# Expert weights fetched as pairs of slices, two neighbouring rows of DRAM per partition, with the gather and the transposes reading every second column

## The chip, the cores and the metric

One NeuronCore of a Trainium2 chip. The metric is the device time of one execution in microseconds; the kernel before takes 1547.8 us (median of 3 runs, 1546.68 to 1548.04).

## The reference

Two transformer blocks over 256 tokens of width 1024, all in float32. The first has window attention, retention and a convolutional feed-forward; the second has differential and banded attention and then the part that the change touches, a mixture of 32 experts of which each token takes 4:

```
logits = t @ w_router + b_router            # t: 256 x 1024
top_val, top_idx = lax.top_k(logits, 4);  gate_w = softmax(top_val)
for each expert e, over the tokens that chose it:
    hb = x_e @ w_exp_in[e] + b_exp_in[e]    # w_exp_in[e]: 1024 x 2048, 8 MB
    g = min(hb[:, :1024], 7);  u = clip(hb[:, 1024:], -7, 7)
    a = g * sigmoid(1.702 * g) * (u + 1)
    y_e = a @ w_exp_out[e] + b_exp_out[e]   # w_exp_out[e]: 1024 x 1024, 4 MB
y[token] = sum over its 4 experts of gate_w * y_e
```

## The kernel before

The kernel is written engine by engine, each with its own list of instructions, held together by semaphores. Everything up to the router takes about 580 us of the span; then a loop runs over the 32 experts in an order that the device works out itself (`order`, sorted by the number of tokens and then mixed). All of the second part's expert weights pass through one buffer: `win` holds eight slices `win[:, k, :]` of 2048 columns, `wout` eight slices of 1024 columns. Slice k of `win` holds rows 128k to 128k+127 of the expert's matrix, one row on each partition (L311 and L312), and comes by one transfer of 1 MB; a slice of `wout` is 0.5 MB.

SP issues all these transfers. For expert 0 it sends sixteen at once (L384 to L387), as soon as the attention part has left the memory. After that `expert` (L393) refills each slice as soon as it is consumed: it waits until PE has counted `gu_part` (for `win`, L400) or `y_part` (for `wout`, L403) once more, and sends the slice of the next expert to the place that has come free (L401, L404). So SP runs up to one whole expert ahead of PE, and the order in its queue is win 0 to 7, wout 0 to 7, win 0 to 7 of the next expert, and so on.

PE does for an expert, in `one_pass` (L942): the bias and eight slices of the first product (`gu`, L855; L873 waits for the slice's own semaphore, L863 are the matmuls, with the gathered tokens `xT` as the stationary operand and the weights moving), a part of the gather for the next expert (`gather`, L841; L846: the stationary operand is `h1`, 128 of its 1024 columns for each k, the moving one a selection matrix `picks`), transposes for the way back (L883), transposes of the activations `a` (`turn_a`, L886; L891), eight slices of the second product (`second`, L894; L897 waits, L902 are the matmuls), and the addition to the tokens (`combine`, L916 or L925). Each slice is counted on `gu_part` (L878) or `y_part` (L906) behind its last matmul.

Tokens come in blocks (`GROUPS`, L36): an expert with up to 32 tokens has one block of 32, up to 64 one block of 64, beyond that both. In this input 19 experts have the small block, 9 the large, and 4 both. An fp32 matmul is shown as two instructions; a slice of `win` is 8 of them with either block, and 16 with both. DVE and ACT make `picks`, the copies of the gathered tokens and the swiglu (L1816 to L1823, L1335, L1339, L1348) beside it.

Of the kernel before, what the change touches and what calls it, by code (L numbers as in the profile page):

```python
# [16 lines left out]
P = 128  # L17
D = 1024
SEQ = 256
T = SEQ // P  # L20
KD = D // P
# [10 lines left out]
SLOTS = TRIO * XS  # L32
# [89 lines left out]
def program(nc, ins, out):  # L122
# [2 lines left out]

    with ExitStack() as ctx:
        s = {n: ctx.enter_context(nc.semaphore(n)) for n in EVENTS}
        win_in = [ctx.enter_context(nc.semaphore(f"win{k}_in")) for k in range(KD)]
        wout_in = [ctx.enter_context(nc.semaphore(f"wout{k}_in")) for k in range(KD)]


        ring_mem = ctx.enter_context(nc.sbuf_tensor("ring_mem", [P, 3 * 4096], F32))
# [24 lines left out]
        def carve(mem, places):  # L157
# [18 lines left out]
        win = big_mem[:, 0:KD * 2 * FE].rearrange("p (k n) -> p k n", k=KD)  # L176
        wout = big_mem[:, KD * 2 * FE:].rearrange("p (k n) -> p k n", k=KD)
# [16 lines left out]
        at = sum(int(np.prod(m2[n].shape[1:])) for n in ("score", "turned", "qaT", "kaT", "va", "qbT", "kbT", "vb", "gateT"))  # L194
        toep_flipped = big_mem[:, at:at + BAND_HEADS * SEQ].rearrange("p (h k) -> p h k", h=BAND_HEADS)
        moe = carve(ring_mem, [
            ("xT", (KD, SLOTS)), ("g", (TRIO * QW,)), ("sig", (TRIO * QW,)), ("u", (TRIO * QW,)),
            ("a", (TRIO * QW,)), ("y", (TRIO * QW,)), ("pairs", (E, E)), ("part", (SEQ,)), ("chosen", (T, 4 * E))])
# [8 lines left out]
        h1 = h  # L207
# [44 lines left out]
        ident = stay[:, IDENT:IDENT + P]  # L252
# [4 lines left out]
        ps = ctx.enter_context(nc.psum_tensor("ps", [P, 8, 512], F32))  # L257
# [50 lines left out]

        cw = ins["conv_w"][0].rearrange("w (f p) -> (w f) p", p=P)
        mix1_cols = [(0, 512), (512, 256), (768, 512), (1280, 512), (1792, 512), (2304, 512)]  # L310
        win_x = ins["w_exp_in_2"].rearrange("l e (k p) n -> (l e) k p n", p=P)  # L311
        wout_x = ins["w_exp_out_2"].rearrange("l e (k p) n -> (l e) k p n", p=P)  # L312


        @block.sync
        def _(sp):
# [64 lines left out]
                sp.dma_start(moe["bias"][E * part:E * (part + 1), 0:2 * FE], ins["b_exp_in_2"][0]).then_inc(s["bias_in"], 16)  # L381
            sp.dma_start(moe["bias"][0:E, 2 * FE:], ins["b_exp_out_2"][0]).then_inc(s["bias_in"], 16)
            sp.wait_ge(s["merged_ready"], KD)
            for k in range(KD):  # L384
                sp.dma_start(win[:, k, :], win_x[0, k]).then_inc(win_in[k], 16)
            for k in range(KD):
                sp.dma_start(wout[:, k, :], wout_x[0, k]).then_inc(wout_in[k], 16)  # L387

            sp.wait_ge(s["counts_ready"], 1)
            done = sp.alloc_register("sp_done")  # L390
# [2 lines left out]
            def expert(before, cur):  # L393

                more = sp.value_load(further[0:1, 1, before], min_val=0, max_val=PASSES - 1)
                sp.reg_add(done, done, more)
                others = sp.snap(done, min_val=0, max_val=2 * TURNS)
                sp.reg_add(done, done, 1)
                for k in range(KD):
                    sp.wait_ge(s["gu_part"], KD * others + 1 + k)  # L400
                    sp.dma_start(win[:, k, :], win_x[cur, k]).then_inc(win_in[k], 16)  # L401
                for k in range(KD):
                    sp.wait_ge(s["y_part"], KD * others + 1 + k)  # L403
                    sp.dma_start(wout[:, k, :], wout_x[cur, k]).then_inc(wout_in[k], 16)  # L404

            expert(slice(0, 1), 1)
            sp.wait_ge(s["order_ready"], 1)
# [28 lines left out]
        def _(pe):  # L436
            mm = nc.tensor.matmul
# [119 lines left out]
            for g in range(2):  # L557
                for k in range(KD):
                    for z in range(2):
                        mm(ps[HEAD * z:HEAD * (z + 1), 2, SEQ * g:SEQ * (g + 1)], cols8[1][:, k, HEAD * g:HEAD * (g + 1)], hT[:, k, :],  # L560
                           start=(k == 0), stop=(k == KD - 1))
            for t in range(T):
                for k in range(KD):
                    last = mm(ps[:, 3, P * t:P * (t + 1)], hT[:, k, P * t:P * (t + 1)], cols8[1][:, k, P:2 * P],
                              start=(k == 0), stop=(k == KD - 1))
# [68 lines left out]
            for t in range(T):  # L634
                last = mixed(0, t, 4, KD)
# [45 lines left out]
            for k in range(NF - 4, NF):  # L681
                pe.wait_ge(s[f"lo{k % 4}"], NF // 2 + k // 4 + 1)
                last = down(k, 0)
# [157 lines left out]
            def gather(lo, hi, bank=7):  # L841

                for k in range(lo, hi):
                    c = SLOTS * (k % EARLY)
                    for t in range(T):
                        last = mm(ps[:, bank, c:c + SLOTS], h1[:, t, P * k:P * (k + 1)], moe["picks"][:, t, :], start=(t == 0), stop=(t == T - 1))  # L846
                if hi in (EARLY, KD):
                    last.then_inc(s["gather_ps"], 1)

# [5 lines left out]
            def gu(blocks, landed_all, tokens_all):  # L855

                def each(at, m, stationary, weights, start, stop):
                    w = D * m // P
                    bank = 4 + at // XS
                    for q in range(P // m):  # L860
                        for f in range(2 if m > XS else 1):
                            out = ps[m * q:m * (q + 1), bank + f, :] if m > XS else ps[m * q:m * (q + 1), bank, :].rearrange("p (f n) -> p f n", f=2)
                            last = mm(out, stationary, weights[:, f, w * q:w * (q + 1)] if m > XS else weights[:, :, w * q:w * (q + 1)], start=start, stop=stop)  # L863
                    return last

                if len(blocks) > 1:
                    pe.wait_ge(s["xT_ready"], tokens_all)
                for at, m in blocks:
                    each(at, m, own[:, 0:m], bias_gu, True, False)
                for k in range(KD):  # L870
                    if k == EARLY:
                        pe.wait_ge(s["xT_ready"], tokens_all)
                    pe.wait_ge(win_in[k], landed_all)  # L873
                    for b, (at, m) in in_turn(blocks, k):
                        last = each(at, m, moe["xT"][:, k, at:at + m], win[:, k, :].rearrange("p (f n) -> p f n", f=2), False, k == KD - 1)
                        if k == KD - 1 and b < len(blocks) - 1:
                            last.then_inc(s["gu_early"], 1)
                    last.then_inc(s["gu_part"], 1)  # L878
# [7 lines left out]
            def turn_a(at, m):  # L886

                w = D * m // P
                for c in range(w // P):
                    place = ps[:, 5, P * c:P * (c + 1)] if m > XS else ps[:, 4 + at // XS, SEQ + P * c:SEQ + P * (c + 1)]  # L890
                    last = nc.tensor.transpose(place, moe["a"][:, KD * at + P * c:KD * at + P * (c + 1)], ident)  # L891
                last.then_inc(s["aT_ps"], 1)

            def second(blocks, landed_all):  # L894

                for k in range(KD):
                    pe.wait_ge(wout_in[k], landed_all)  # L897
                    for b, (at, m) in in_turn(blocks, k):
                        w, n = D * m // P, m // 16
                        aT = aT_all[:, KD * at:KD * at + w].rearrange("p (c q m) -> p c q m", q=P // m, m=m)  # L900
                        for q in range(P // m):
                            last = mm(ps[m * q:m * (q + 1), 4 + at // XS, 0:w], aT[:, k % n, k // n, :], wout[:, k, w * q:w * (q + 1)],  # L902
                                      start=(k == 0), stop=(k == KD - 1))
                        if k == KD - 1 and b < len(blocks) - 1:
                            last.then_inc(s["y_early"], 1)
                    last.then_inc(s["y_part"], 1)  # L906
# [1035 lines left out]
```

## Time and profile before

| | |
|---|---|
| median of 3 runs | 1547.8 us (1546.68 to 1548.04) |
| the profiled execution | 1548.02 us, its span 1545.4 us |
| PE busy | 1358.8 us (88%) |
| DVE, ACT, POOL busy | 425.2, 331.7, 121.4 us |
| moved by DMA | 494.35 MB, mean 320 GB/s |
| of it expert weights | 256 transfers of 1 MB and 256 of 0.5 MB |

The trace shows one execution. Times are microseconds from the start of the span; the span is shorter than the execution by what lies before its first and behind its last instruction. PE is the matmul side of TensorE, PEld its weight loads, which run beside the matmuls. SPq and ACTq are the queues that issue transfers. The stretch from 583 us to 1530 us is the loop over the experts, over 60% of the span; the layer norm and the output follow in the last 15 us.

### The profile page before, as it was taken

How to read it: one execution, taken by the hardware profiler on the slowest of the kernel's cores; microseconds unless marked ns; L12 is line 12 of the kernel's file. 1: busy time of each engine (PE TensorE's matmuls, PEld its weight loads, DVE VectorE, ACT ScalarE, POOL GpSimd, SP SyncE). 2: the span in 40 equal slices, each digit the busy share in tenths (PEclk: the TensorE clock that was granted, in tenths of full speed). 3: DMA queues.
4: the chain of work that ended last, by engine and by line, in shares of the span. 5: the costliest groups of instructions: out<-in, count | busy, mean ns of one | idle time of the engine just before them, and what ended most of it. 6: DMA issues, size and time to landing. Idle time of an engine off the chain costs nothing.

```text
span 1545.4 us, 25866 instructions
## 1 busy us (share of the span) xinstructions
PE 1358.8 (88%) x9234; PEld 788.9 (51%) x9235; DVE 425.2 (28%) x892; ACT 331.7 (21%) x638; POOL 121.4 (8%) x56
## 2 busy tenths in 40 slices
PE   7998999998899998998988788988889988879874
PEld 5554999887789744442343243343323433333421
DVE  0336687753543262111021111111111111111112
ACT  2233566534555211000010010010000101000000
POOL 0000112005665000000000000000000000000000
PEclk9999999999999999999999998999999999999997
DMA  9341366855343198999999999999999999999995
GB/s 334 131 142 55 109 179 188 312 191 183 111 164 134 68 368 326 370 419 418 415 419 418 417 417 418 419 416 420 418 417 417 418 420 415 420 418 417 417 418 241
DMA packets 150051, 494.35 MB, mean 320 GB/s; under 512 B 11665, under 2 KB 59137, under 8 KB 117025
## 3 DMA queue, kind: packets, MB, share of 16 engines
q1 hardware_dynamic: 148531, 491.52, 81.1%
q10 hardware_dynamic: 1486, 2.34, 0.4%
q8 instruction: 25, 0.41, 0.1%
q14 instruction: 9, 0.07, 0.0%
HBM read 492.76 MB, written 1.06 MB: 320 GB/s over the span
## 4 chain that ended last, share of the span: by engine, by line
PE 58%; DMA 19%; SPq 12%; DVE 4%; issue 3%; ACT 3%; ACTq 0%; DVEq 0%
DMA big_mem<-in_w_exp_in 13%; PE ps L863 12%; SPq L404 8%; PE ps L902 6%; DMA big_mem<-in_w_exp_out 6%; PE ps L644 5%; PE ps L645 5%; PE ps L646 5%; PE ps L846 5%; PE ps L477 4%; SPq L401 3%; PE ps L774 2%; PE ps L782 2%; PE ps L616 2%; PE ps L668 1%
## 5 line engine op out<-in xcount | busy, mean ns | idle before, releaser
L863 PE MATMUL ps<-big_mem,ring_mem 128*32 128x512 f32 (+1 forms) x2304 | 391.9, 647 | 63.4 <-DMA big_mem<-in_w_exp_in 63.4
L863 PEld LDWEIGHTS ps<-big_mem,ring_mem 128*32 128x32 f32 (+1 forms) x2304 | 107.5, 124 | 321.3 <-issue 197.0
L902 PE MATMUL ps<-big_mem,x 128*32 128x256 f32 (+1 forms) x1888 | 183.3, 430 | 12.8 <-DMA big_mem<-in_w_exp_out 8.1
L644 PE MATMUL ps<-hT_hi,w_hi 128*128 128x256 f32 x600 | 172.0, 287 | 1.1 <-DVE hT_lo L1422 1.1
L645 PE MATMUL ps<-hT_lo,w_hi 128*128 128x256 f32 x600 | 171.1, 285 | 0.0
L646 PE MATMUL ps<-hT_hi,w_lo 128*128 128x256 f32 x600 | 171.0, 285 | 0.0
L846 PEld LDWEIGHTS ps<-ring_mem,h 128*128 128x128 f32 x1056 | 135.6, 202 | 64.6 <-issue 63.5
L846 PE MATMUL ps<-ring_mem,h 128*128 128x96 f32 x1056 | 153.5, 292 | 0.6 <-DVE ring_mem L1775 0.6
L1816 DVE TENSOR_SCALAR ring_mem<-ps 128x256 f32<-128x256 f32 (+1 forms) x36 | 18.7, 520 | 438.8 <-PE ps L863 438.8
L902 PEld LDWEIGHTS ps<-big_mem,x 128*32 128x32 f32 (+1 forms) x1888 | 69.6, 115 | 112.7 <-issue 64.8
L1335 ACT ACTIVATE ring_mem<-ring_mem 128x256 f32<-128x256 f32 (+1 forms) x36 | 17.7, 493 | 497.9 <-DVE ring_mem L1816 497.9
L644 PEld LDWEIGHTS ps<-hT_hi,w_hi 128*128 128x128 f32 x600 | 116.6, 194 | 3.8 <-issue 2.3
L645 PEld LDWEIGHTS ps<-hT_lo,w_hi 128*128 128x128 f32 x600 | 116.6, 194 | 0.0
L646 PEld LDWEIGHTS ps<-hT_hi,w_lo 128*128 128x128 f32 x600 | 116.5, 194 | 0.0
L1339 ACT ACTIVATE ring_mem<-ps 128x480 f32<-128x480 f32 x66 | 32.5, 492 | 354.2 <-PE ps L846 354.2
L429 POOL TENSOR_TENSOR w_lo<-ring_mem,w_hi 128x1024 fp32r<-128x1024 f32 x38 | 91.2, 2408 | 126.4 <-ACT w_hi L1222 126.4
L1832 DVE COPY ring_mem<-ps 128x256 f32<-128x256 f32 (+1 forms) x36 | 18.4, 520 | 269.4 <-PE ps L902 269.4
L477 PE MATMUL ps<-ring_mem,hT 128*128 128x512 f32 x128 | 56.0, 595 | 0.0
L1806 DVE TENSOR_SCALAR ring_mem<-stay,posb,gate 128x128 f32<-128x128 f32 x72 | 21.4, 344 | 103.6 <-PE ps L846 85.5
L1222 ACT ACTIVATE w_hi<-ring_mem 128x1024 fp32r<-128x1024 f32 x39 | 40.9, 1056 | 33.7 <-PE ps L646 27.7
L1148 ACT ACTIVATE w_hi<-ring_mem 128x1024 fp32r<-128x1024 f32 x44 | 44.9, 1050 | 0.0
L424 POOL TENSOR_TENSOR w_lo<-ring_mem,w_hi 128x1024 fp32r<-128x1024 f32 x11 | 26.8, 2441 | 219.6 <-ACT w_hi L1148 219.6
(284 smaller groups left out, 1328.0 us busy)
## 6 DMA issues: line engine op xcount, KB each, us to landing
big_mem<-in_w_exp_in SPq DMA_DIRECT2D x256, 1024.0 KB, 19.4
big_mem<-in_w_exp_out SPq DMA_DIRECT2D x256, 512.0 KB, 19.0
ring_mem<-in_w_in SPq DMA_DIRECT2D x15, 2048.0 KB, 8.0
ring_mem<-in_w_up SPq DMA_DIRECT2D x44, 512.0 KB, 4.9
ring_mem<-in_w_down SPq DMA_DIRECT2D x5, 2048.0 KB, 8.7
ring_mem<-in_w_out SPq DMA_DIRECT2D x4, 2048.0 KB, 8.7
ring_mem<-in_w_branch_a SPq DMA_DIRECT2D x1, 2048.0 KB, 7.5
ring_mem<-in_w_branch_b SPq DMA_DIRECT2D x1, 2048.0 KB, 7.4
```

The costliest lines, as they stand in the source:

```text
L401: sp.dma_start(win[:, k, :], win_x[cur, k]).then_inc(win_in[k], 16)
L404: sp.dma_start(wout[:, k, :], wout_x[cur, k]).then_inc(wout_in[k], 16)
L429: nc.gpsimd.tensor_tensor(split_piece(w2_lo, p), piece(p), split_piece(w2_hi, p).bitcast(F32), ALU.subtract).then_inc(s["m2_lo"], 1)
L477: last = mm(ps[:, bank + t, :], hT[:, k, P * t:P * (t + 1)], cols8[n % 3][:, k, :], start=(k == 0), stop=(k == KD - 1))
L644: mm(out, hi, x_hi, start=start, stop=False)
L645: mm(out, hi, x_lo, start=False, stop=False)
L646: return mm(out, lo, x_hi, start=False, stop=stop)
L846: last = mm(ps[:, bank, c:c + SLOTS], h1[:, t, P * k:P * (k + 1)], moe["picks"][:, t, :], start=(t == 0), stop=(t == T - 1))
L863: last = mm(out, stationary, weights[:, f, w * q:w * (q + 1)] if m > XS else weights[:, :, w * q:w * (q + 1)], start=start, stop=stop)
L902: last = mm(ps[m * q:m * (q + 1), 4 + at // XS, 0:w], aT[:, k % n, k // n, :], wout[:, k, w * q:w * (q + 1)], start=(k == 0), stop=(k == K ...
L1148: run(quarter(w_hi, b), up_slot[u][:, :, g, :], ACT.Copy).then_inc(s[f"hi{b}"], 1)
L1222: run(split_piece(w2_hi, p), piece(p), ACT.Copy).then_inc(s["m2_hi"], 1)
```

## The change

Two neighbouring rows of an expert's matrix go to the same partition. Slices 2k and 2k+1 are filled by one transfer: partition p gets rows 256k + 2p and 256k + 2p + 1, which are adjacent in DRAM, and puts them in slice 2k and slice 2k+1, which are adjacent in its memory. A transfer is thus 2 MB for `win` and 1 MB for `wout`, and there are four of each per expert. SP waits for both slices of a pair to be consumed, PE waits once per pair, and the semaphores are one per pair. Since slice 2k now holds the even rows of its 256 and slice 2k+1 the odd ones, the gather takes every second column of `h1`, and the transposes of `a` every second column of `a`. No instruction of PE, DVE or ACT that computes is added or removed.

```diff
-        win_in = [ctx.enter_context(nc.semaphore(f"win{k}_in")) for k in range(KD)]
-        wout_in = [ctx.enter_context(nc.semaphore(f"wout{k}_in")) for k in range(KD)]
+        win_in = [ctx.enter_context(nc.semaphore(f"win{k}_in")) for k in range(KD // 2)]
+        wout_in = [ctx.enter_context(nc.semaphore(f"wout{k}_in")) for k in range(KD // 2)]
...
-        win_x = ins["w_exp_in_2"].rearrange("l e (k p) n -> (l e) k p n", p=P)
-        wout_x = ins["w_exp_out_2"].rearrange("l e (k p) n -> (l e) k p n", p=P)
+        win_x = ins["w_exp_in_2"].rearrange("l e (k p j) n -> (l e) k p j n", p=P, j=2)
+        wout_x = ins["w_exp_out_2"].rearrange("l e (k p j) n -> (l e) k p j n", p=P, j=2)
...
-            for k in range(KD):
-                sp.dma_start(win[:, k, :], win_x[0, k]).then_inc(win_in[k], 16)
-            for k in range(KD):
-                sp.dma_start(wout[:, k, :], wout_x[0, k]).then_inc(wout_in[k], 16)
+            for k in range(KD // 2):
+                sp.dma_start(win[:, 2 * k:2 * k + 2, :], win_x[0, k]).then_inc(win_in[k], 16)
+            for k in range(KD // 2):
+                sp.dma_start(wout[:, 2 * k:2 * k + 2, :], wout_x[0, k]).then_inc(wout_in[k], 16)
...
-                for k in range(KD):
-                    sp.wait_ge(s["gu_part"], KD * others + 1 + k)
-                    sp.dma_start(win[:, k, :], win_x[cur, k]).then_inc(win_in[k], 16)
-                for k in range(KD):
-                    sp.wait_ge(s["y_part"], KD * others + 1 + k)
-                    sp.dma_start(wout[:, k, :], wout_x[cur, k]).then_inc(wout_in[k], 16)
+                for k in range(KD // 2):
+                    sp.wait_ge(s["gu_part"], KD * others + 2 + 2 * k)
+                    sp.dma_start(win[:, 2 * k:2 * k + 2, :], win_x[cur, k]).then_inc(win_in[k], 16)
+                for k in range(KD // 2):
+                    sp.wait_ge(s["y_part"], KD * others + 2 + 2 * k)
+                    sp.dma_start(wout[:, 2 * k:2 * k + 2, :], wout_x[cur, k]).then_inc(wout_in[k], 16)
...
-                        last = mm(ps[:, bank, c:c + SLOTS], h1[:, t, P * k:P * (k + 1)], moe["picks"][:, t, :], start=(t == 0), stop=(t == T - 1))
+                        last = mm(ps[:, bank, c:c + SLOTS], h1[:, t, SEQ * (k // 2) + k % 2:SEQ * (k // 2 + 1):2], moe["picks"][:, t, :], start=(t == 0), stop=(t == T - 1))
...
-                    pe.wait_ge(win_in[k], landed_all)
+                    if k % 2 == 0:
+                        pe.wait_ge(win_in[k // 2], landed_all)
...
-                    last = nc.tensor.transpose(place, moe["a"][:, KD * at + P * c:KD * at + P * (c + 1)], ident)
+                    last = nc.tensor.transpose(place, moe["a"][:, KD * at + SEQ * (c // 2) + c % 2:KD * at + SEQ * (c // 2 + 1):2], ident)
...
-                    pe.wait_ge(wout_in[k], landed_all)
+                    if k % 2 == 0:
+                        pe.wait_ge(wout_in[k // 2], landed_all)
```

## Rows read from the trace of the kernel before

**Rows 1.** The page, part 2: the span in 40 slices of 38.6 us.

```profile
PE   7998999998899998998988788988889988879874
DMA  9341366855343198999999999999999999999995
GB/s 334 131 142 55 109 179 188 312 191 183 111 164 134 68 368 326 370 419 418 415 419 418 417 417 418 419 416 420 418 417 417 418 420 415 420 418 417 417 418 241
big_mem<-in_w_exp_in SPq DMA_DIRECT2D x256, 1024.0 KB, 19.4
big_mem<-in_w_exp_out SPq DMA_DIRECT2D x256, 512.0 KB, 19.0
```

**Rows 2.** Grouped waits of PE, 622 to 1526 us: us in total, times, longest.

```profile
PE ps L863 <- DMA big_mem<-in_w_exp_in: 63.4, 73, 1.5
PE ps L891 <- ACT hT L1343: 14.7, 31, 0.7
PE ps L902 <- DMA big_mem<-in_w_exp_out: 7.0, 12, 0.6
```

**Rows 3.** Stretches of the expert loop; last columns: PEclk, DMA share, GB/s.

```profile
622.00:1526.00 904.00, 778.88 (x5792) 334.43 (x5788) 120.43 (x333) 74.65 (x166) 0.00 (x0) 0.96 1.02 417
580.00:590.00 10.00, 9.73 (x53) 5.93 (x54) 6.11 (x11) 2.27 (x3) 0.00 (x0) 0.89 0.31 109
610.00:620.00 10.00, 4.83 (x28) 2.23 (x32) 1.62 (x5) 0.41 (x1) 0.00 (x0) 0.81 0.81 318
620.00:630.00 10.00, 10.00 (x79) 3.95 (x72) 1.71 (x5) 0.42 (x1) 0.00 (x0) 0.85 0.79 297
```

**Rows 4.** Timeline of PE, experts 30 and 31: slices of `win` as they land.

```profile
1476.14 1.07 PE L863 MATMUL ps<-big_mem,ring_mem 128*32 128x512 f32 x8 [1.42 <-DMA big_mem<-in_w_exp_in]
...
1506.26 1.06 PE L863 MATMUL ps<-big_mem,ring_mem 128*32 128x512 f32 x8 [1.42 <-DMA big_mem<-in_w_exp_in]
1508.75 1.07 PE L863 MATMUL ps<-big_mem,ring_mem 128*32 128x512 f32 x8 [1.42 <-DMA big_mem<-in_w_exp_in]
1511.23 1.93 PE L863 MATMUL ps<-big_mem,ring_mem 128*32 128x512 f32 x8 [1.42 <-DMA big_mem<-in_w_exp_in]
```

**Rows 5.** Stretches with one size of row each; the last column is GB/s.

```profile
274.00:282.00 8.00, 8.00 (x69) 8.00 (x68) 6.52 (x11) 4.19 (x9) 2.40 (x1) 1.00 1.02 414
550.00:564.00 14.00, 14.00 (x34) 6.12 (x33) 12.12 (x11) 0.20 (x1) 0.00 (x0) 1.00 1.01 422
566.00:576.00 10.00, 7.89 (x48) 4.43 (x48) 8.61 (x32) 3.65 (x8) 0.00 (x0) 0.96 1.02 410
5.00:10.00 5.00, 0.63 (x2) 0.29 (x2) 1.47 (x4) 2.39 (x5) 0.00 (x0) 1.00 1.00 340
```

**Rows 6.** The page, part 3: packets by size.

```profile
DMA packets 150051, 494.35 MB, mean 320 GB/s; under 512 B 11665, under 2 KB 59137, under 8 KB 117025
```

**Rows 7.** Timeline, expert 0 on PE and the refill that opens the stream.

```profile
583.38 0.65 PE L863 MATMUL ps<-ring_mem 128*64 128x512 bf16 x4 [0.27 <-issue]
612.72 0.69 PE L846 MATMUL ps<-ring_mem,h 128*128 128x96 f32 x4
620.84 7.61 SPq L401 DMA_DIRECT2D big_mem<-in_w_exp_in  x8
```

**Rows 8.** Timeline of PE, an expert with both blocks and the one behind it.

```profile
1180.63 16.22 PE L863 MATMUL ps<-big_mem,ring_mem 128*32 128x512 f32 x92
1220.34 0.61 PE L863 MATMUL ps<-ring_mem 128*32 128x512 bf16 x4 [1.78 <-issue]
1220.71 8.59 PE L863 MATMUL ps<-big_mem,ring_mem 128*32 128x512 f32 x64
1233.88 3.66 PE L902 MATMUL ps<-big_mem,x 128*32 128x256 f32 x64
```

**Rows 9.** L401 in five short stretches, us from issue to landing.

```profile
L401 SPq DMA_DIRECT2D big_mem<-in_w_exp_in x1: 348/348/348, 620.8 to 620.8; - x1
DMA to landing us min/median/max: 4.8/4.8/4.8
...
L401 SPq DMA_DIRECT2D big_mem<-in_w_exp_in x1: 333/333/333, 1222.8 to 1222.8; - x1
DMA to landing us min/median/max: 7.3/7.3/7.3
...
DMA to landing us min/median/max: 10.0/10.0/10.0
...
DMA to landing us min/median/max: 15.2/15.2/15.2
```

**Rows 10.** The last expert on PE: timeline, and the granted clock in one stretch.

```profile
1513.81 1.94 PE L863 MATMUL ps<-big_mem,ring_mem 128*32 128x512 f32 x8 [0.64 <-DMA big_mem<-in_w_exp_in]
1518.69 1.06 PE L863 MATMUL ps<-big_mem,ring_mem 128*32 128x512 f32 x8 [0.88 <-DMA big_mem<-in_w_exp_in]
1524.33 2.80 PE L902 MATMUL ps<-big_mem,x 128*32 128x256 f32 x48
1528.85 0.64 PE L902 MATMUL ps<-big_mem,x 128*32 128x256 f32 x8 [0.59 <-DMA big_mem<-in_w_exp_out]
...
1510.00:1515.00 5.00, 3.13 (x16) 0.43 (x16) 0.00 (x0) 0.00 (x0) 0.00 (x0) 0.55 1.01 419
```

**Rows 11.** Timeline, one small expert: the gather's loads and the bf16 bias matmul.

```profile
1008.21 0.41 PE L863 MATMUL ps<-ring_mem 128*32 128x512 bf16 x4 [1.78 <-issue]
1017.11 2.31 PEld L846 LDWEIGHTS ps<-ring_mem,h 128*128 128x128 f32 x20 [0.84 <-issue]
1017.11 2.47 PE L846 MATMUL ps<-ring_mem,h 128*128 128x96 f32 x20
```

## The prediction

> **What bounds the kernel now.** I first read the page's 40 slices [rows 1]: from slice 17 on (650 us) the DMA engines are at 9 tenths and move 415 to 420 GB/s without a break, and what they move is 256 + 256 slices of expert weights, 12.6 MB per expert, 403 MB in all. PE is busy too (7 to 9 tenths), so the second view is the grouped waits of that stretch [rows 2]: PE waits 63.4 us for `win` and 7.0 us for `wout`, more than for any other engine; no transfer waits long enough to leave a hole. The third is the table by stretches [rows 3]: 417 GB/s as a mean over 904 us, with holes only before: 109 GB/s in 580 to 590 us (expert 0 has begun, nothing is consumed yet) and 318 and 297 GB/s around 620 us. So the time is: the point near 621 us at which the stream is refilled, then 30 experts at the pace of the DMA engines, then the tail. The pace is in the timeline of experts 30 and 31 [rows 4]: PE gets the third `win` slice of one at 1476.14 us and of the next at 1506.26: 30.12 us per expert, and 30 of them are 903.6 us. Slices of `win` land every 2.485 us (1506.26, 1508.75, 1511.23). What is left is eight of `wout`: (30.12 - 8 x 2.485) / 8 = 1.28 us each.
>
> **What a row costs.** A `win` slice is 128 rows of 8 KB, a `wout` slice 128 rows of 4 KB; each of the 16 DMA engines carries 8 rows of either. Twice the bytes take 1.205 us more, so half a MB is 1.205 us of moving and 1.28 - 1.205 = 0.075 us that doesn't depend on size: 9 ns per row and engine. The table of stretches agrees [rows 5]: 8 KB rows alone (550 to 564 us) go at 422 GB/s, 4 KB rows alone (566 to 576 us) at 410, 2 KB rows (5 to 10 us, with 4 KB rows of `x` among them) at 340. Is the fixed part one per row or one per transfer? Transfers of `w_down` carry 2 MB in 4 KB rows (274 to 282 us): 414 GB/s, 5.07 us each, 4.82 of it moving, so 0.25 us over 32 rows: 8 ns per row. Had it been 0.075 us per transfer, they would run at 2.097 MB / 4.895 us = 428 GB/s. It is per row. The page counts 150051 - 117025 = 33026 packets of 8 KB or more [rows 6], and 256 `win` slices are 32768 rows: a row of 8 KB is one packet today.
>
> **The change, part by part.** (1) Two neighbouring DRAM rows go to one partition, where slices 2k and 2k+1 also lie side by side, so both ends of a pair are one run of 16 KB (`win`) or 8 KB (`wout`). Rows carried per expert and engine fall from 128 to 64. A `win` pair then takes 4 x 1.205 + 0.075 = 4.895 us instead of 4.97, a `wout` pair 2.485 instead of 2.56, 0.075 us less each; eight pairs 0.60 us per expert; with the 8 ns of `w_down` it would be 0.51. I take 0.58, over 30 experts **-17.4 us** (bounds -15.4 and -18). No row of the trace is 16 KB long; the nearest, 8 KB, is the fastest of all.
>
> (2) SP waits for two consumed slices before it refills. Where the queue is full this costs nothing: the last refills wait some 15 us for their turn (15.2 us to landing at 1275.2 us against 4.8 on an empty queue [rows 9]). Where it is empty it costs one slice of PE's time. That is so at 620.84 us, expert 1's first slice, which opens the stream; the eight issues take 7.61 us [rows 7], so the next comes about 1.0 us later: **+1.0 us**. Behind SP's wait only its own later refills are queued.
>
> (3) The next place is behind the four experts with both blocks (64 and 32 tokens). PE takes 39.7 us for such a pass (its first matmul at 1180.63, that of the next expert at 1220.34) against the stream's 30.1 [rows 8]. The first refill after it lands 7.3 us after its issue at 1222.8 us and 10.0 at 1431.0 (the two between are 8.8 and 9.1), against 4.8 on the empty queue of 620.8 [rows 9]. Spare is thus 2.5, 4.0, 4.3 and 5.2 us. The change takes from it: one slice of PE (0.86 us, since 64 matmuls here take 8.59 us, the first slice more), one `wout` slice at the end of the expert before (64 matmuls of L902 take 3.66 us, so 0.46), and 0.6 us because the stream itself is quicker: 1.9 to 2.0 us. The narrowest is barely covered: **+0.2 us**, bounds 0 and +4 (four times a slice, were the cover gone).
>
> (4) PE waits for pairs. In the stream that only moves PE within time it has to spare. At the end it shows [rows 10]: `win`'s last slice is seen at 1518.69 and takes 1.06 us; with pairs two slices follow, +1.06 us, or +1.9 if they run at the lower clock (in 1510 to 1520 us slices take 1.61 to 1.94 us instead of 1.06, and the granted clock was 0.55 in 1510 to 1515, so partly 1.2 GHz, after PE had sat idle more than half of the time). The swiglu then starts later, L902 at T-3.5 instead of T-4.5 us before the last landing T (1528.85); six slices of 0.46 us fit in that, and behind T there are two instead of one: +0.46. At the lower clock it is +1.4. I take **+0.7 us**.
>
> (5) The gather reads `h1`, and the transposes read `a`, at every second column (L846, L891). The trace has no fp32 weight load with a step of 8 bytes. Its nearest row is the same load packed: 20 in 2.31 us, 115 ns apart [rows 11]; its matmuls take 2.47 us, so a pair of load and matmul goes by the load. A second near row is the bias matmul (L863, bf16 read out of fp32 pairs at 4 bytes' step), four in 0.41 us with no sign of a stall. Bounds 0 and +115 ns for each of the 32 loads per expert (+3.7 us); I take 0, since in the stream even half of that would be hidden. The Trainium skill (SBUF — State Buffer, the note on cachelines) says that reads stay at full rate while at least two of them fall in one 16-byte line; at a step of 8 bytes exactly two do, so by that page the sum keeps its 0. (6) Half the semaphores and half of PE's waits go: nothing, as PE isn't the bound, at most a few tenths behind the four long experts.
>
> **Sum:** -17.4 + 1.0 + 0.2 + 0.7 = -15.5 us. The profiled execution took 1548.02 us (span 1545.4), 0.2 over the median of 1547.8: 1548.0 - 15.5 = 1532.5, as a median **1532.3 us**.
>
> **Rivals.**
> A. *The rows aren't joined.* If the transfer is cut at the old row, or the engines cut at 8 KB, the fixed part stays or is only halved (for `wout` alone). Then 1548 + 1.9 = 1549.7 us, or 1541 with half. For it: only rows up to 8 KB are seen. Against: both sides are one run, and at 8 KB a row is still one packet. The Trainium skill (DMA: Bandwidth & Descriptors, why small descriptors are slow) gives about 3 cycles per packet and calls joining worth it only up to 256 bytes; by that rule no gain would be seen, but the cadence here shows 9 ns on rows of 4 and 8 KB. Chance 0.10 (0.06 none, 0.04 half).
> B. *Slower: the strided weight load takes double.* Then 3.7 us are added to each expert on PE. Nothing hides it ahead of the stream: the first gather (32 loads) and expert 0's pass, +7.4 us. Behind each of the four long experts 3.7 + 2.0 us meet spares of 2.5 to 5.2: +3.2, +1.7, +1.4, +0.5, and once or twice as much again where a 64-token expert follows (30.0 us on PE without a wait, 583.38 to 613.4) [rows 7]; at the end about +2. In sum 7.4 + 6.8 + 2 = 16 to 30: 1549 to 1562 us, 1555 taken. It decides from about a doubling on; a load up to half longer leaves the forecast within 8 us. Chance 0.09.
> C. *16 KB rows are slower.* If 16 engines that read 64 KB apart get in each other's way, and pairs go at the 410 GB/s of 4 KB rows, an expert takes 30.7 us: 1565 us. For it: nothing but that no such row is seen; against: 422 at 8 KB is over 410 at 4 KB. Chance 0.04.
> D. *The gain is partly given back*: the queue runs dry behind the long experts and at the lower clock. All upper bounds of (2) to (4) and the lower of (1): -15.4 + 2.0 + 4 + 1.4 = -8.0, 1540 us. Chance 0.06.
>
> **How the numbers follow.** Forecast 0.71, A 0.10, B 0.09, C 0.04, D 0.06. The forecast's own range is 1529 to 1537. Low end 1528.5; the high end reaches over D and A to 1551 and leaves out most of B and C and a little below, some 0.13 to 0.15. This kernel can be told from no change beyond about 0.2% (3.1 us; its three runs spread by 1.4). Faster: 0.71 + 0.06 + 0.04 = 0.81; same: A without gain and the edge of B, 0.08; slower: 0.11.
>
> **What would show it.** The page's count of packets: 65536 rows of expert weights become 32768, so 150051 falls to some 117,000 or a little less (half as many completions go too), while those of 8 KB or more stay at 33,000. GB/s in the stretches from 700 us on: 426 instead of 417; `win` landing one pair in 4.9 us. Expert to expert 29.5 us instead of 30.1. L846's loads still 2.31 us for 20. No slice under 415 GB/s behind the long experts. The forecast is wrong if the rate stays at 417, if L846's loads lengthen, or if the stream opens much later than 622 us.

## The result, and the profile after

The changed kernel takes **1533.5 us** (median of 4 runs, 1533.0 to 1535.5) against 1547.7 (4 runs, 1546.7 to 1548.0): a ratio of 0.991, 95% interval 0.990 to 0.9925. Forecast were 1532.3 us and 1528.5 to 1551. The profiled execution took 1533.0 us, its span 1530.4; the pieces below add up in spans, 1545.4 before and 1530.4 now.

The page's 40 slices (38.3 us each here), packets and transfers answer to [rows 1] and [rows 6]:

```profile
PE   7998999998899999898898887998879988889874
DMA  9441366855343197899999999999999999999995
GB/s 337 149 127 55 110 182 188 316 192 169 127 165 112 60 395 288 363 428 427 424 412 430 425 425 430 427 408 428 427 425 427 410 428 424 427 427 425 427 427 248
DMA packets 113187, 494.33 MB, mean 323 GB/s; under 512 B 7569, under 2 KB 55041, under 8 KB 80161
big_mem<-in_w_exp_in SPq DMA_DIRECT2D x128, 2048.0 KB, 23.2
big_mem<-in_w_exp_out SPq DMA_DIRECT2D x128, 1024.0 KB, 22.6
```

The stream goes at 427 GB/s where it was 418. There are 36,864 packets fewer: 32,768 because 65,536 rows were joined in pairs, and 4,096 under 512 B (11665 - 7569) that went with 256 transfers. Packets of 8 KB or more are 113187 - 80161 = 33026, as before: 16,384 of 16 KB and 16,384 of 8 KB stand where 32,768 of 8 KB stood, so a run of 16 KB is one packet. And three slices stand out that didn't before: 412, 408 and 410 GB/s.

The timeline of PE in experts 30 and 31 answers to [rows 4] (pairs of `win` as they land) and [rows 10]:

```profile
1464.13 3.56 PE L863 MATMUL ps<-big_mem,ring_mem 128*32 128x512 f32 x16 [2.97 <-DMA big_mem<-in_w_exp_in]
...
1493.65 2.58 PE L863 MATMUL ps<-big_mem,ring_mem 128*32 128x512 f32 x16 [2.62 <-DMA big_mem<-in_w_exp_in]
1498.55 3.42 PE L863 MATMUL ps<-big_mem,ring_mem 128*32 128x512 f32 x16 [2.31 <-DMA big_mem<-in_w_exp_in]
1503.45 1.93 PE L863 MATMUL ps<-big_mem,ring_mem 128*32 128x512 f32 x16 [1.49 <-DMA big_mem<-in_w_exp_in]
...
1513.37 1.07 PE L904 MATMUL ps<-big_mem,x 128*32 128x256 f32 x16 [0.54 <-DMA big_mem<-in_w_exp_out]
```

A pair lands every 4.90 us (1493.65, 1498.55, 1503.45), and the second pair of one expert comes 29.52 us behind that of the one before (1464.13, 1493.65): 0.60 us less than the 30.12 of before. The last `wout` pair is seen at 1513.37, the span ends 17.0 us later; before it was 1528.85 and 16.5.

Expert 0's first product as PE's timeline has it, then the refills by SP and the first one's way to landing, answer to [rows 7] and [rows 9]:

```profile
581.73 13.95 PE L863 MATMUL ps<-big_mem,ring_mem 128*64 128x512 f32 x64
...
585.41 10.63 SPq L401 DMA_DIRECT2D big_mem<-in_w_exp_in  x4
620.63 5.82 SPq L401 DMA_DIRECT2D big_mem<-in_w_exp_in  x4
...
L401 SPq DMA_DIRECT2D big_mem<-in_w_exp_in x1: 348/348/348, 620.6 to 620.6; - x1
DMA to landing us min/median/max: 7.9/7.9/7.9
...
L401 SPq DMA_DIRECT2D big_mem<-in_w_exp_in x1: 337/337/337, 799.1 to 799.1; - x1
DMA to landing us min/median/max: 7.8/7.8/7.8
...
DMA to landing us min/median/max: 9.6/9.6/9.6
```

The refill that opens the stream needs 7.9 us on an empty queue. Behind the four long experts (those with both blocks of tokens) the first refill needs 7.8, 7.8, 7.7 and 9.6: three times it hardly found anything ahead of it, which didn't happen once before (7.3 to 10.0 us against 4.8).

So the 15.0 us between the two spans fall into these pieces:

| piece | forecast | measured |
|---|---|---|
| start of expert 0's first slice (583.86, now 581.73) | 0 | -2.1 |
| from there to the refill that opens the stream (36.98, now 38.90) | +1.0 | +1.9 |
| pace, 30 experts | -17.4 | -18.0 (30 x 0.60) |
| behind the long experts | +0.2 | +2.7 (from the opening to the last landing 908.0, now 892.7, less the pace) |
| tail | +0.7 | +0.5 |
| sum | -15.5 | -15.0 |

The fourth line is what is left of the loop without the pace. The landings show where it arises. From `wout`'s last landing of one expert to that of the next it is 30.12 us before and 29.52 now, but where the first refill behind a long expert stands between them it is 29.85, 30.99, 30.90 and 29.51: 0.3, 1.5, 1.4 and 0 us lost, 3.2 in all; before, none was. About 0.6 us less than before (0.9 instead of 1.5) is lost while the first long expert runs, near 760 us; what makes that gap, in both kernels, no trace shows.

### The profile page after: what moved, and what is told of

Same layout as the page of the kernel before. It is cut to its first block, busy times and chain, and to the rows that moved or that the text cites. A ratio compares the mean times of both kernels' runs of the same rounds, so it can differ in the third digit from the quotient of the medians.

```text
span 1530.4 us, 24974 instructions
## 1 busy us (share of the span) xinstructions
PE 1345.6 (88%) x9234; PEld 796.6 (52%) x9235; DVE 425.2 (28%) x892; ACT 331.8 (22%) x638; POOL 121.4 (8%) x56
## 2 busy tenths in 40 slices
DMA packets 113187, 494.33 MB, mean 323 GB/s; under 512 B 7569, under 2 KB 55041, under 8 KB 80161
## 4 chain that ended last, share of the span: by engine, by line
PE 59%; DMA 32%; DVE 4%; ACT 3%; issue 2%; SPq 0%; ACTq 0%; DVEq 0%
DMA big_mem<-in_w_exp_in 24%; PE ps L863 15%; DMA big_mem<-in_w_exp_out 8%; PE ps L904 7%; PE ps L644 5%; PE ps L645 5%; PE ps L646 5%; PE ps L477 4%; PE ps L846 3%; PE ps L774 2%; PE ps L782 2%; PE ps L616 2%; PE ps L669 1%; PE ps L668 1%; PE ps L670 1%
## 5 line engine op out<-in xcount | busy, mean ns | idle before, releaser
L863 PE MATMUL ps<-big_mem,ring_mem 128*32 128x512 f32 (+1 forms) x2304 | 377.6, 631 | 68.5 <-DMA big_mem<-in_w_exp_in 68.5
L863 PEld LDWEIGHTS ps<-big_mem,ring_mem 128*32 128x32 f32 (+1 forms) x2304 | 111.7, 124 | 311.4 <-issue 197.3
L429 POOL TENSOR_TENSOR w_lo<-ring_mem,w_hi 128x1024 fp32r<-128x1024 f32 x38 | 91.2, 2408 | 126.3 <-ACT w_hi L1224 126.3
L1643 DVE SCALAR_TENSOR_TENSOR big_mem<-ps,cols,big_mem 128x255 f32<-128x255 f32 (+1 forms) x88 | 38.4, 478 | 20.5 <-ACT big_mem L1172 16.3
```

What stands on the lines that cost most here:

```text
L429: nc.gpsimd.tensor_tensor(split_piece(w2_lo, p), piece(p), split_piece(w2_hi, p).bitcast(F32), ALU.subtract).then_inc(s["m2_lo"], 1)
L1643: last = v.scalar_tensor_tensor(c, ps[:, 4 + u, SEQ * g:SEQ * (g + 1) - i], cols[:, bass.ds(tap + f, 1)], c, ALU.mult, ALU.add)
```

## The experiments

Each ratio is to the kernel before on the same chip, with its 95% interval. The granted clock is that of the profile's stretches.

**1. Is the fixed cost one per row, or one per transfer?** The pairs stay, the rows go back to their old places:

```diff
-        win_x = ins["w_exp_in_2"].rearrange("l e (k p j) n -> (l e) k p j n", p=P, j=2)
+        win_x = ins["w_exp_in_2"].rearrange("l e (k j p) n -> (l e) k p j n", p=P, j=2)
```

(`wout` alike; gather and transposes packed again.)

> Transfers, waits and semaphores in pairs as in the changed kernel, but with the old assignment of rows: a transfer of 2 MB brings two blocks of 128 rows, so a partition gets two separate rows of 8 KB (4 KB for wout), and gather and transposes read packed columns. Theory (the fixed cost is 9 ns per row on each DMA engine): the stream keeps its 417 to 418 GB/s and 30.1 us per expert, all that was saved is gone and the coarser waits stay: about 1548 + 1.0 (opening) + 0.5 (tail) + 0 to 1 behind the long experts = 1549.5 to 1550.5 us, packets in all about 146,000. Rival (the fixed cost is one per transfer, 0.075 us): 426 to 427 GB/s, 1533 us.

Measured: 1548.6 us, ratio 1.0013 (1.0003 to 1.0022). The page's rates are the old ones:

```profile
GB/s 333 126 147 55 109 176 188 313 190 180 113 164 133 68 367 315 367 418 419 415 418 419 417 417 419 418 416 419 418 417 417 419 419 416 419 418 417 409 419 246
```

It is per row: half as many transfers of twice the size save nothing, and what is left is the price of the coarser waits, 1.9 us over the 1546.7 of the kernel before on the same chip, as forecast.

**2. What do the strided reads and the spread rows cost alone?** Slice by slice as in the kernel before, with the new places of the rows:

```diff
-                    sp.dma_start(win[:, k, :], win_x[cur, k]).then_inc(win_in[k], 16)
+                    sp.dma_start(win[:, k, :], win_x[cur, k // 2, :, k % 2, :]).then_inc(win_in[k], 16)
```

> Transfers, waits and semaphores slice by slice as in the kernel before, but slice 2k takes the even and slice 2k+1 the odd rows of their 256 (8 KB rows 16 KB apart in DRAM), and gather and transposes read every second column. It prices the strided reads and the spread rows alone. Theory: gather loads 20 in 2.43 us instead of 2.31, hidden by the stream; rate 417 to 418 GB/s; 1547.5 to 1549 us. Rival (the strided reads or the spread rows cost time of their own that the pairs pay for): over 1551 us, with a rate under 415 GB/s or fresh dips behind the long experts.

Measured: 1548.95 us (10 runs, 1546.8 to 1550.1), ratio 1.0011 (1.0002 to 1.0021): at the upper end of the theory. The rate in undisturbed stretches is 418 GB/s. There is one fresh dip, the stretch 1010 to 1020 us behind the second long expert at 340 GB/s. That expert had met the lower clock in its first product (0.72 in 965 to 970 us), which it hadn't in the trace before (1.00), so this dip can't be laid to the strided loads alone.

**3. Does the coarse first refill make the dips?**

```diff
-                for k in range(KD // 2):
+                for j in range(2):
+                    sp.wait_ge(s["gu_part"], KD * others + 1 + j)
+                    sp.dma_start(win[:, j, :], win_x[cur, 0, :, j, :]).then_inc(win_in[KD // 2 if j else 0], 16)
+                for k in range(1, KD // 2):
                     sp.wait_ge(s["gu_part"], KD * others + 2 + 2 * k)
```

> The changed kernel, but the first pair of win goes as two transfers of one slice each (8 KB rows, 16 KB apart), each refilled when its own slice is consumed and waited for by itself; the other seven pairs stay. It costs 8 rows more per engine and expert, 0.075 us, 2.3 us over 30 experts. Theory (what the changed kernel loses behind three of the four long experts and at the opening is that its first refill waits for a second slice, 1.0 us at the opening and up to 1.4 us three times): the opening comes 1.0 us sooner, the refills behind the long experts 1.4 us, the three dips (404 to 412 GB/s in a slice of 38 us) shrink by half or more: 1531 us. Rival (the dips come from the quicker stream alone and an early first slice doesn't reach them): 1535 us, dips as in the changed kernel.

Measured: 1533.0 us, ratio 0.9914 (0.990 to 0.993): between the two, and not to be told from the changed kernel. Its trace shows that both terms of the theory were there and paid each other off. The page's rates, and the timeline (PE's pairs in experts 30 and 31):

```profile
GB/s 337 143 134 55 110 177 191 318 193 162 135 164 112 56 385 299 374 426 425 424 423 428 424 424 427 425 423 426 426 423 424 427 425 424 426 425 424 413 427 238
...
619.22 2.04 SPq L403 DMA_DIRECT2D big_mem<-in_w_exp_in  x2
...
1467.51 3.64 PE L868 MATMUL ps<-big_mem,ring_mem 128*32 128x512 f32 x16 [1.26 <-DMA big_mem<-in_w_exp_in]
...
1497.11 1.93 PE L868 MATMUL ps<-big_mem,ring_mem 128*32 128x512 f32 x16 [1.41 <-DMA big_mem<-in_w_exp_in]
1502.01 3.47 PE L868 MATMUL ps<-big_mem,ring_mem 128*32 128x512 f32 x16 [2.97 <-DMA big_mem<-in_w_exp_in]
```

The three dips are gone (423, 423, 427), one of 413 came behind the fourth long expert. An expert takes 29.60 us (1467.51, 1497.11), the 0.08 that were reckoned, 2.4 us over 30. The stream opens at 619.22 instead of 620.63, and from there to `win`'s last landing both kernels take 882.8 us: what was saved behind the long experts is just what the eight more rows cost. Of the 1.4 us at the opening 0.9 were given back in the tail (27.9 us from `win`'s last landing to the end instead of 27.0), where the last pair ran at the lower clock (3.47 us instead of 1.93).

**4. Fours instead of pairs, for the rivals' prices.** Four neighbouring rows go to one partition by one transfer. That changes three things at once: the row length (32 KB), the gather's step (16 bytes) and the grain of the refills; the next two kernels take the last two one by one.

```diff
-        win_x = ins["w_exp_in_2"].rearrange("l e (k p j) n -> (l e) k p j n", p=P, j=2)
+        win_x = ins["w_exp_in_2"].rearrange("l e (k p j) n -> (l e) k p j n", p=P, j=4)
...
+                        last = mm(ps[:, bank, c:c + SLOTS], h1[:, t, 4 * P * (k // 4) + k % 4:4 * P * (k // 4 + 1):4], moe["picks"][:, t, :], start=(t == 0), stop=(t == T - 1))
```

> The changed kernel with win in fours: four neighbouring rows (32 KB) per partition in one transfer of 4 MB, refilled after four slices, the gather reading every fourth column; wout stays in pairs. Theory: the fixed part is saved once more, 2 x 0.075 us per expert, -4.5 us over 30, rate 429 to 430 GB/s in undisturbed stretches; against it the opening comes two slices later (+2 us), the tail has two slices more (+1), and behind each of the four long experts the first refill comes 1.7 to 2.7 us later (+7 to +11): 1539 to 1543 us with deeper dips. Rival (no loss from coarser refills, size alone counts): 1529 us. Of the gather's loads: 20 in 2.4 to 2.5 us if a step of 16 bytes is no worse than 8, 4.6 us if each then costs a line of its own; the second would add 3.6 us to each pass and make it 1560 us or more.

Measured: 1598.2 us, ratio 1.034 (1.032 to 1.035): the slow load's branch (1560 us or more), and well inside it. At that step the loads take twice as long (timeline, one expert):

```profile
722.36 4.74 PEld L846 LDWEIGHTS ps<-ring_mem,h 128*128 128x128 f32 x20 [0.81 <-issue]
```

Where its stream still runs undisturbed, the row's price shows once more: the first `wout` pair of two neighbouring experts lands at 653.88 and 683.25 us, 29.37 apart, 0.15 less than with pairs, for 256 rows fewer.

**5. The gather's step alone.** Runs of 16 KB in pairs as in the changed kernel, but dealt out in fours, so that the gather reads every fourth column (its line as in experiment 4).

```diff
+        win_x = ins["w_exp_in_2"].rearrange("l e (g p h j) n -> (l e) g p h j n", p=P, h=2, j=2)
...
+                    sp.dma_start(win[:, 2 * k:2 * k + 2, :], win_x[cur, k // 2, :, k % 2, :, :]).then_inc(win_in[k], 16)
```

> Transfers, sizes and waits exactly as in the changed kernel (runs of 16 KB, pairs), but the rows are dealt in fours, so that the gather reads every fourth column (16 bytes) and the runs stand 32 KB apart in DRAM. It prices a slow strided load alone, the prediction's rival B. In the kernel with fours the 20 loads took 4.74 us, so each pass gets (4.74 - 2.43) / 20 x 32 = 3.7 us more of PE. Theory (rival B's working): +16 to +30 us over the changed kernel, 1549 to 1562 us. Rival (the stream hides nearly all of it, and the 1598 us of the fours came from the coarse refills): under 1545 us. A second rival (hardly any of it is hidden: 32 x 3.7 = 118 us): over 1580 us.

Measured: 1585.2 us, ratio 1.025 (1.023 to 1.026): far over the theory. By the time it falls to the second rival (over 1580 us), but not by that rival's working, in which hardly any of 118 us is hidden: +52 us over the changed kernel came through. It is the prediction's rival B come true, at about twice its price (+16 to +30). Grouped lines of 620 to 1560 us, and a 64-token pass from the timeline:

```profile
L863 PE MATMUL ps<-big_mem,ring_mem 128*32 128x512 f32 x1472 | 173.0, 614 | 6.7 <-DMA big_mem<-in_w_exp_in 6.7
L846 PEld LDWEIGHTS ps<-ring_mem,h 128*128 128x128 f32 x984 | 239.6, 328 | 56.1 <-issue 56.1
...
706.49 0.65 PE L863 MATMUL ps<-ring_mem 128*64 128x512 bf16 x4 [0.21 <-issue]
720.85 4.98 PE L846 MATMUL ps<-ring_mem,h 128*128 128x96 f32 x20
728.69 8.35 PE L904 MATMUL ps<-big_mem,x 128*64 128x512 f32 x32
741.09 0.41 PE L863 MATMUL ps<-ring_mem 128*32 128x512 bf16 x4
...
620.00:1565.00 945.00, 904.62 (x5840) 479.45 (x5840) 120.32 (x333) 71.88 (x166) 0.00 (x0) 0.89 0.96 400
```

PE waits for `win` 6.7 us in all instead of 68.5: it has become the bound. The pass takes 34.6 us without a wait for DMA (706.49 to 741.09) against 30.0 [rows 7], 4.6 more: the loads are 3.7, and the second product, of which nothing was changed, takes 8.35 instead of 7.09 us; a part of both fills time in which PE stood idle before. The granted clock is 0.85 while that second product runs and 0.89 over the loop, 0.98 in the changed kernel, so parts of it ran at 1.2 instead of 2.4 GHz. The Trainium skill (SBUF — State Buffer, the note on cachelines) gives the rule of two reads per 16-byte line, and the traces agree: 2.31 us for 20 loads packed, 2.43 at two per line, 4.74 at one; what the same note adds, that fp32 may be strided by up to four elements for free, they contradict at four (4.74).

**6. The grain of the refills alone.** Rows and gather as in the changed kernel, four slices of `win` per transfer.

```diff
+        win_x = ins["w_exp_in_2"].rearrange("l e (g i p j) n -> (l e) g p i j n", i=2, p=P, j=2)
...
+                    sp.wait_ge(s["gu_part"], KD * others + 4 + 4 * k)
```

> Rows as in the changed kernel (16 KB runs, gather at every second column), but one transfer brings four slices of win, and is refilled and waited for as a whole. It prices the coarser refill alone. Theory: opening two slices later (+2 us), tail +1, behind each of the four long experts two slices later than the pair (0.9 to 1.4 us each, +1.9 to +2.8 four times, +8 to +11): 1544 to 1548 us at 427 GB/s in undisturbed stretches, with dips under 400 GB/s behind the long experts. Rival (fours are slow because of coarse refills in every pass): over 1560 us.

Measured: 1559.0 us, ratio 1.0067 (1.0046 to 1.0087), 25 us over the changed kernel and 11 to 15 over the theory, just short of the rival's 1560. But the place is the theory's, not the rival's: from 660 us on the page's rates are whole but for four slices.

```profile
GB/s 332 150 122 54 112 192 187 293 188 183 131 141 163 72 331 325 393 426 425 427 369 428 424 428 427 424 372 427 425 425 429 348 426 427 427 427 424 363 427 214
...
754.89 22.82 PE L863 MATMUL ps<-big_mem,ring_mem 128*32 128x512 f32 x128 [0.25 <-DMA big_mem<-in_w_exp_in]
...
1512.95 0.41 PE L863 MATMUL ps<-ring_mem 128*32 128x512 bf16 x4 [0.28 <-issue]
1515.95 3.64 PE L863 MATMUL ps<-big_mem,ring_mem 128*32 128x512 f32 x32 [2.59 <-DMA big_mem<-in_w_exp_in]
```

Those four (369, 372, 348, 363, slices of 38.9 us) lack (427 - rate) / 427 of 38.9 us each, 5.3, 5.0, 7.2 and 5.8: 23 us. What the theory had left out is on PE's side: in the last expert PE is ready at 1512.95 and waits until 1515.95 for its first four slices. An expert that starts later for such a wait refills later too. It is so at all four long experts: each begins its first product (754.89 us for the first of them) right as its four slices land, 9.8 us behind the last `wout` landing of the expert before, where the changed kernel begins 6.2 to 6.5 us behind it. As their pass is longer than the stream's period, the 3.3 to 3.7 us aren't made up before the refill behind it; four times that is what the theory lacked.

**7. `wout` alone.** From the changed kernel, `win` goes back to its old rows, slice by slice, and the gather to packed reads:

```diff
-            for k in range(KD // 2):
-                sp.dma_start(win[:, 2 * k:2 * k + 2, :], win_x[0, k]).then_inc(win_in[k], 16)
+            for k in range(KD):
+                sp.dma_start(win[:, k, :], win_x[0, k]).then_inc(win_in[k], 16)
```

> Only wout goes in pairs (8 KB rows; transposes of a at every second column); win keeps its slices of 8 KB rows, its waits and the packed gather. Theory: half of the saving, 0.075 us four times, 0.30 us per expert, -9.0 us over 30 experts; the opening and the refills behind the long experts hang on win's slices and cost nothing, the tail has one wout slice more (+0.5); rate 422 GB/s; 1538 us. Rival (win's longer rows carry most of the saving): over 1541 us.

Measured: 1541.2 us (6 runs, 1537.5 to 1542.8), ratio 0.9958 (0.994 to 0.997): by the time on the rival's side, by the trace on the theory's. The profiled execution is one of the two shortest (1537.65 us), at 422 GB/s, and an expert takes 29.82 us, 0.30 less:

```profile
1465.90 1.06 PE L863 MATMUL ps<-big_mem,ring_mem 128*32 128x512 f32 x8 [1.16 <-DMA big_mem<-in_w_exp_in]
...
1495.72 1.07 PE L863 MATMUL ps<-big_mem,ring_mem 128*32 128x512 f32 x8 [1.15 <-DMA big_mem<-in_w_exp_in]
```

So by this trace each matrix brings half of the pace's gain. Why four of its six runs are 3.5 to 5 us longer, no trace shows.

**8. A better variant?** `win` in transfers of 1, 2, 2, 2 and 1 slices:

```diff
+        win_groups = ((0, 1), (1, 2), (3, 2), (5, 2), (7, 1))
...
+                for i, (k, n) in enumerate(win_groups):
+                    sp.wait_ge(s["gu_part"], KD * others + k + n)
```

> The changed kernel with win in five transfers of 1, 2, 2, 2 and 1 slices: the first and the last slice have packed rows of 8 KB and packed gather columns, the three pairs between are as in the changed kernel. It has the early first refill of the kernel with the split first pair, and one slice instead of two behind win's last landing. Cost: 8 rows more per engine and expert, 0.08 us, 2.4 us over 30. Theory (as measured there: opening 1.4 us sooner, 2.4 us less lost behind the long experts; new: tail 1 to 2 us shorter): 2.4 - 1.4 - 2.4 - 1.5 = -3 us against the changed kernel, 1530.5 us. Rival (the holes move elsewhere, the last slice is hidden by wout): 1533 us, no difference.

Measured: 1533.3 us (1532.4 to 1534.1), ratio 0.9906 (0.989 to 0.992). Beside it on the same chip:

> The changed kernel once more, beside the one before and the variant with 1, 2, 2, 2, 1 slices, for its time and for where its first 32 us go: in the trace at hand the stretch of L466 took 14.05 us against 15.96 in the kernel before, though nothing of it was changed. Theory (that stretch differs from run to run, or with the place of the code, and not with this change): 1533 to 1536 us, ratio 0.991. Rival (the 2 us belong to the change): L466 again 14.05 us.

Measured: 1535.3 us (1533.0 to 1537.4), ratio 0.9912 (0.9895 to 0.993). The medians are 2.0 us apart, and the two can't be told apart; the variant's rates behind the long experts are 424 to 417 GB/s. The second trace of the changed kernel has the same pace, and shows all four dips (407, 406, 407, 411). It opens the stream at 621.85 and sees `win`'s last pair at 1506.95, 885.1 us later instead of 882.8: the table's fourth line is +2.7 us in one execution and +5.0 in another of the same kernel. By the landings this one lost 0.6, 1.6, 1.7 and 1.6 us behind the four long experts.

**9. The first 32 us.** The chain of work shows the 64 matmuls of L466, from about 15 us on, as 15.96 us in the trace before and 14.05 in both of the changed kernel, which has nothing to do with it.

> The kernel before once more, for one question: the stretch of L466 (64 matmuls near 15 to 31 us), untouched by the change, took 15.96 us in its trace and 14.05 in both traces of the changed kernel, but also 16.4 and 14.05 us in variants that differ from each other only in the rows of the experts. Theory (the stretch has two lengths that come with the execution): it can be 14.05 here. Rival (each build has its own): 15.9 to 16 us again.

Measured: 15.62 us. Shorter than the 15.9 that the rival had, and far from 14.05. It was long in both traces of the kernel before and in experiments 1 (16.38), 2 (15.88) and 4 (15.94), and 14.05 in experiments 3, 5, 6, 7 and the variant of 8. It doesn't go with pairs (1 and 4 have them), so the change doesn't make it by what it does. Both kernels that were traced twice kept theirs within 0.4 us, which speaks for the build, but two kernels don't settle it. It is most of the -2.1 us in the table's first line; in the second trace of the changed kernel the 64 matmuls took 14.05 us again, but began later, and expert 0 (583.06) was only 0.8 us ahead of the kernel before.

## Why the prediction was right

**The bound and the pace.** Right, and shown from both sides: with rows joined an expert takes 29.52 us, with `wout`'s alone 29.82, with neither 30.12, and bigger transfers of the old rows leave the rate at 418 GB/s. The fixed part was taken from two slice sizes of the same eight rows, and the transfers of `w_down` were the row that decided between row and transfer. Forecast 0.58 us per expert, measured 0.60: to go below the cadence's 0.60 towards the 0.51 of `w_down` was needless caution. Rivals A and C fall with it: the rows are joined, and 16 KB rows are no slower (427 GB/s).

**The opening.** +1.0 forecast, +1.9 measured. The mean spacing of the eight issues (1.0 us) was taken for the second slice's time. It took 1.7 us, at a mean granted clock of 0.89 in this pass: the refill is issued 3.8 us behind expert 1's first matmul, and 2.1 in experiment 3, which takes the wait for the second slice away. The other 0.2 us are expert 0's pass, 35.1 instead of 34.9 us, with its slower gather, for which part (5) took nothing.

**Behind the long experts.** The one step that failed: +0.2 us forecast, "the narrowest is barely covered", +2.7 and in another execution +5.0 measured. Three terms were too small, and the spares were read too large.

The stream's own speed counts for two experts there, not one: when PE starts on a long expert, all but the first slices of its weights and all of the next expert's are still to come, so the stream is ahead by 2 x 0.60 us at the refill in question, not by 0.6. The second slice took 0.86 us, as was taken, only behind the fourth long expert; behind the first it took 1.4: SP's issue at 799.15 us comes 3.5 us behind the start of the product at 795.64, for one slice it had been 2.1 (797.58 to 799.72). The granted clock of that pass is 0.92, of the one behind the fourth long expert 1.00. With 0.46 for `wout` and 0.2 for the slower gather of two passes the spare shrinks by 2.7 us at the full clock and by 3.3 with 1.4 for the slice. The landings bear that out: the refill was issued 6.3, 6.7, 4.9 and 7.5 us before the last landing of what was queued, and is now issued 2.5, 1.4, 1.4 and 4.7 before it, 3.8, 5.3, 3.4 and 2.7 us less. The 5.3 has a term that isn't in this sum: the second long expert's own pass met the lower clock in its first product now (the stretch of 5 us below, 0.66) and took 48.3 us, where before it took 46.6 at 1.00.

```profile
955.00:960.00 5.00, 5.00 (x24) 1.27 (x24) 1.21 (x6) 0.00 (x0) 0.00 (x0) 0.66 0.99 419
```

And what has to be left isn't nothing. The 0.3, 1.5 and 1.4 us lost at 2.5, 1.4 and 1.4 us of lead all point to a lead of 2.8 us below which the stream loses (an estimate from these three sums). Before, there were thus 2.1 to 4.7 us to spare, not 2.5 to 5.2. The second trace fits (lead 2.1, 1.1, 1.2, 1.2, lost 0.6, 1.6, 1.7, 1.6): there PE began on the fourth long expert 8.0 us behind the last `wout` landing instead of 6.2, and the pass behind it had 0.92 of the clock, so this refill came late too. The mechanism was named, and its bound of +4 held in the trace on which the table rests, but not in the second. The sentence that no slice would fall under 415 GB/s was wrong.

**A row misread.** The same step says that PE takes 39.7 us for a long pass, from 1180.63 [rows 8]. That row is where the cut of the timeline begins, in the middle of the first product. The pass begins at 1172.34 us in the chain of work and takes 48 us. The forecast's sum didn't use it (the spares came from the landings). But with 39.7 us a long pass looks shorter than it is to whoever asks what PE has left, and that is rival B's question.

**Rival B's price.** It was never tested by the change, since a step of 8 bytes costs 5% of a load (2.43 us for 20, rival at 4.6). Experiment 5 tested it: a doubling costs 52 us, not 16 to 30. A sum over PE's passes with 48 us for a long one would have shown it. From expert 1 on, 19 small passes of 20.3 us, 8 of 30.0 and 4 of 48 are 818 us beside the stream's 885. With the 3.7 us of the loads for each of the 31 it is 933, and with the 4.6 measured, in which the lower clock has its part, 960: PE is the bound over the loop. The trace of experiment 5 has 946 us from expert 1's start to the end of its last pass.

**The tail.** +0.7 forecast, +0.5 measured; the lower clock that was feared there came in experiment 3 and in the second trace of the changed kernel (3.60 us for the last pair instead of 1.93), and in each cost about 0.9 us.

**A compensation.** Of the three losses two were larger than forecast (1.9 us for 1.0, 2.7 for 0.2) and the tail a little smaller; the pace gave 0.6 us more. Together the loop and the tail make -12.9 us, not -15.5. The start that came 2.1 us early, of which the forecast knew nothing, brought the sum to -15.0. That the total came so near is luck; the range would have held without it.

## What to carry to other kernels

Where DMA is the bound, subtract two row lengths with the same number of rows per engine: what doesn't scale is the price of a row, and a transfer with more rows of the same length tells whether it belongs to the row or to the transfer. Then join rows as long as the engine that reads the data doesn't pay for the step: here a step of 8 bytes cost a weight load 5%, one of 16 bytes doubled it. A coarser refill is free only while the queue is full: look for the passes that are longer than the stream's period, count what their first refill has to spare, and subtract the time that the quicker stream gains over all that is queued, not over one pass, and what a pass takes longer when it meets the lower clock (1.7 us of 46.6 here).

## What the runs showed of the hardware that was not expected

- The price of a row didn't change with its length: joining 4 KB rows to 8 (`wout`, experiment 7) saves 0.30 us per expert, 512 rows on 16 engines or 9.4 ns each; joining 8 to 16 (`win`) saves the other 0.30, again for 512 rows; 16 to 32 (experiment 4) saves 0.15, for 256 rows, 9.4 ns each. The rates are 418, 422 and 427 GB/s for the first three.
- fp32 weight loads of 128 columns: 115 ns apart packed, 121 at a step of 8 bytes, 237 at 16.
- In the kernel with those slower loads (experiment 5) the granted clock was 0.89 over the loop where it had been 0.98, though PE was busy more of the time (905 of 945 us against 767 of 891), and matmuls that weren't touched grew by 18% (7.09 to 8.35 us for 32): a load that lengthens cost more than its own length here. Sizes, waits and the untouched matmuls were as in the changed kernel; how the loads bring the clock down no run shows.
